# Level 0 of a triangular inverse moved from its own code into the loop over levels, with the side work re-placed

## The reference, cut to what matters

```python
def step(S, inp):
    r_t, w_t, k_t, v_t, kk_t, a_t = inp
    s_kk = jnp.einsum('zbhvk,zbhk->zbhv', S, kk_t)
    S = (S * w_t[..., None, :] - s_kk[..., None] * (kk_t * a_t)[..., None, :]
         + v_t[..., :, None] * k_t[..., None, :])
    return S, jnp.einsum('zbhvk,zbhk->zbhv', S, r_t)
```

```python
y = (y - mu) * lax.rsqrt(var + GN_EPS) * heads(gn_w.astype(f32)) + heads(gn_b.astype(f32))
out = ((y + bonus).reshape(B_, L, D_A) * gate).astype(h.dtype)
```

## Time and profile before

| what | value |
|---|---|
| median of three runs | 2405.79 us |
| the profiled execution's own time | 2401.35 us |
| its span | 2399.4 us |
| mean granted clock of TensorE | 0.983 |
| PE busy | 2243.7 us (94%) |
| DVE busy | 936.9 us (39%) |
| ACT busy | 397.0 us (17%) |

### The profile page before, as it was taken

The page is one execution under the profiler, slowest core; times in us unless marked ns, Lnnn a source line. Parts: engine busy times, 40 slices in busy tenths (PEclk is TensorE's granted clock), DMA queues, the critical chain, the costliest instruction groups (busy, mean ns, idle before and its releaser), DMA issues. The chain is left out here.

```text
span 2399.4 us, 56100 instructions
## 1 busy us (share of the span) xinstructions
PE 2243.7 (94%) x23412; PEld 1282.6 (53%) x23412; DVE 936.9 (39%) x1965; ACT 397.0 (17%) x685; POOL 167.3 (7%) x162
## 2 busy tenths in 40 slices
PE   5998989999888889999999999889998999999997
PEld 2446777777676765544444444545555444444444
DVE  2357666676757621211111111479613111111113
ACT  2022323232323201000000000211312000000001
POOL 1001010100101000000000000000000000000000
PEclk8998999999999999999999999899999999999999
DMA  9981010101000035799999999502036999999995
GB/s 369 386 316 32 2 33 2 32 2 32 13 22 21 2 122 197 268 383 393 395 396 393 394 396 390 193 1 70 1 140 255 395 397 394 393 397 393 392 392 172
DMA packets 181670, 538.56 MB, mean 224 GB/s; under 512 B 12545, under 2 KB 54145, under 8 KB 181410
## 3 DMA queue, kind: packets, MB, share of 16 engines
q1 hardware_dynamic: 175202, 515.16, 55.8%
q0 software_dynamic: 6336, 21.63, 3.8%
HBM read 510.81 MB, written 25.95 MB: 224 GB/s over the span
## 5 line engine op out<-in xcount | busy, mean ns | idle before, releaser
L2108 PE MATMUL ps<-raw,xs 128*64 128x512 f32 x3072 | 673.8, 596 | 4.0 <-PEq L2102 3.9
L2108 PEld LDWEIGHTS ps<-raw,xs 128*64 128x64 f32 x3072 | 217.7, 137 | 431.0 <-issue 429.6
L2120 PE MATMUL ps<-raw,xs 128*32 128x256 f32 x6144 | 342.3, 380 | 3.2 <-PEq L2102 3.2
L2120 PEld LDWEIGHTS ps<-raw,xs 128*32 128x32 f32 x6144 | 195.1, 110 | 134.0 <-issue 10.4
L2299 DVE SCALAR_TENSOR_TENSOR h<-h,ps 128x768 f32<-128x768 f32 x32 | 30.5, 954 | 461.9 <-DVEq L2298 461.9
L1644 DVE COPY_PREDICATED wk<-m,ps 128x128 f32<-128x128 uint8 x360 | 101.4, 352 | 116.4 <-DVEq L1640 116.2
L2426 PE MATMUL ps<-h,raw 128*128 128x512 f32 (+1 forms) x448 | 124.7, 440 | 7.2 <-PEq L2417 7.2
L2227 ACT ACTIVATE h<-ps 128x768 f32<-128x768 f32 x32 | 25.9, 811 | 595.1 <-ACTq L2226 595.1
L900 PE MATMUL ps<-h,wk 128*128 128x512 f32 (+1 forms) x416 | 121.4, 438 | 1.5 <-PEq L1216 1.3
L1030 PE MATMUL ps<-wk 64*64 64x64 f32 x2400 | 102.9, 223 | 14.5 <-PEq L1006 13.8
L1044 PE MATMUL ps<-wk 64*64 64x64 f32 x2400 | 98.5, 219 | 5.0 <-PEq L1006 3.2
(11 more groups left out here) (333 smaller groups left out, 2643.9 us busy)
## 6 DMA issues: line engine op xcount, KB each, us to landing
raw<-in_moe_w_gate SPq DMA_DIRECT2D x64, 2048.0 KB, 18.0
raw<-in_moe_w_up SPq DMA_DIRECT2D x64, 2048.0 KB, 20.0
raw<-in_moe_w_down SPq DMA_DIRECT2D x64, 2048.0 KB, 19.1
wk<-in_mod_w SPq DMA_DIRECT2D x24, 2048.0 KB, 12.1
wk<-in_ev_w_in SPq DMA_DIRECT2D x18, 512.0 KB, 5.3
raw<-in_od_w_in SPq DMA_DIRECT2D x4, 2048.0 KB, 15.2
hrow<-rows SPq DMA_DIRECT2D x10, 512.0 KB, 2.9
ysum<-low SPq DMA_DIRECT2D x10, 512.0 KB
```

Of the source, the lines that this page charges most:

```text
L2108: last = pe.matmul(ps[to:to + CAPS, bank_of(kind, ee)], XS[ee][:, c, 0:CAPS], raw[:, slot(l, 2 * m + c // 4), c % 4, 8 * to:8 * to + 512], ...
L2120: last = pe.matmul(ps[to:to + 32, bank_of(kind, ee) + 1, 0:256], XS[ee][:, c, CAPS:], raw[:, slot(l, 2 * m + c // 4), c % 4, 8 * to:8 * to ...
```

## The change

Level 0 loses its own code. The loop on PE has five turns, for levels 0 to 4, and each turn has 128 tokens of `keys`; so `keys(ST)` moves from ahead of the loop to its last turn. Ahead of the loop stand now only the first three `middle`, which at level 0 multiply with the identity. ACT makes 35 copies of `yw` instead of 30. The wait for the identities moves from DVE to PE, ahead of the first `middle`, and DVE gives the first turn its four counts of `x_new` at once. `TAIL` is spread over levels 0 to 4. For the last pair, and only there, each step of the tail stands behind every third tile (q = 2, 5, ... 23) and not behind the fifth tile of a level.

```diff
--- before.py
+++ after.py
@@ -818,7 +818,7 @@
             halves = ((0, NS), (NS, T))
             Q, K, VV = 0, 1, 2
             QUERY_ENDS = (0, 3, NT)
-            TAIL = ((0, 1), (2, 3), (4, 5), (6,), (7,), ())
+            TAIL = ((0,), (1, 2), (3, 4), (5,), (6, 7), ())
 
             def cells_of(ap, j):
 
@@ -1005,22 +1005,6 @@
 
                             pe.wait_ge(sem(name), n).then_inc(sem(name), -n)
 
-                        def diagonal(ap, lo, hi):
-
-                            return ap[lo:hi, :, :, 0, lo:hi].rearrange("p z h n -> p (z h) n")
-
-                        def first_correct(g):
-
-                            zb = zbank(g)
-                            for k, (lo, hi) in enumerate(HALF):
-                                to, te = HALF[1 - k]
-                                pe.matmul(ps[to:te, zb, 0:4 * HD].rearrange("p (u n) -> p u n", u=4), eye64[lo:hi], diagonal(mat[:, g], lo, hi), start=True, stop=True)
-                            for z in range(2):
-                                for hh in range(2):
-                                    for lo, hi in HALF:
-                                        last = pe.matmul(ps[lo:hi, zb + 1, slotN(z, hh):slotN(z, hh) + HD], mat[lo:hi, g, z, hh, 0, lo:hi], eye64[lo:hi], start=True, stop=True)
-                            last.then_inc(sem("z_ready"), 1)
-
                         def correct(g, both=True):
 
                             zb = zbank(g)
@@ -1064,29 +1048,21 @@
 
                         def keys(tt):
 
-                            at = slice(tt * P, tt * P + P) if isinstance(tt, int) else bass.ds(tt * P, P)
+                            at = bass.ds(tt * P, P)
                             for c in range(KC):
                                 last = pe.matmul(pair(0)[:, at], win[:, c, K], h[:, c, at], start=c == 0, stop=c == KC - 1)
                             last.then_inc(sem("keys_ready"), 1)
 
-                        first_correct(0)
-                        first_correct(1)
+                        pe.wait_ge(sem("invT_reset"), 1).then_inc(sem("invT_reset"), -1)
                         pe.wait_ge(sem("yvar_read"), 1).then_inc(sem("yvar_read"), -1)
+                        middle(0)
+                        middle(1)
                         pe.wait_ge(sem("r_copied"), 1).then_inc(sem("r_copied"), -1)
                         if following:
                             take_weights()
-                            keys(ST)
-                        take("x_new", 2)
-                        first_correct(2)
-                        middle(0)
-                        take("x_new", 2)
-                        first_correct(3)
-                        middle(1)
-                        take("x_new", 2)
-                        first_correct(4)
                         take("yw_copied", 1)
                         middle(2)
-                        with pe.Fori(0, LEVELS - 2) as lev:
+                        with pe.Fori(0, LEVELS - 1) as lev:
                             take("x_new", 4)
                             correct(0)
                             take("yw_copied", 1)
@@ -1330,11 +1306,11 @@
                         y_root()
                         act.sem_inc(sem("yvar_read"), 1)
                         copy_r(0, 1)
-                        for u in range(NZ):
-                            g, w = u % NT, 4 * HD if u < NZ - NT else 2 * HD
+                        for u in range(NZ + NT):
+                            g, w = u % NT, 4 * HD if u < NZ else 2 * HD
                             act.wait_ge(sem("yw_ready"), 1).then_inc(sem("yw_ready"), -1)
                             act.activation(yw[:, g].rearrange("p z h n -> p (z h n)")[:, 0:w], ps[:, mbank(g), 0:w], ACT.Copy).then_inc(sem("yw_copied"), 1)
-                            if u == NZ - NT - 1:
+                            if u == NZ - 1:
                                 act.wait_ge(sem("tail_done"), 1).then_inc(sem("tail_done"), -1)
                                 if following:
                                     copy_raw(K, 0, parts=NT)
@@ -1634,7 +1610,7 @@
                                     n += 1
                             if tt == 0:
                                 old_states()
-                        dve.wait_ge(sem("invT_reset"), 1).then_inc(sem("invT_reset"), -1)
+                        dve.sem_inc(sem("x_new"), 4)
                         for q in range(NZ):
                             g = q % NT
                             dve.wait_ge(sem("z_ready"), 1).then_inc(sem("z_ready"), -1)
@@ -1646,9 +1622,11 @@
                             if q >= NZ - NT:
                                 done(2)
                                 dve.sem_inc(sem("x_new"), 2)
-                            if g == NT - 1:
+                            if following and g == NT - 1:
                                 for k in TAIL[lev]:
                                     tail(k, i)
+                            if not following and q % 3 == 2 and q < 24:
+                                tail(q // 3, i)
                         for lo, hi in ((0, HD), (HD, P)):
                             for g in range(NT):
                                 dve.tensor_copy(mat[lo:hi, g, :, :, 0, lo:hi], xx[P - hi:P - lo, g, :, 0]).then_inc(dve_done, 1)
```

## The result

The changed kernel takes 2418.22 us, the median of five runs from 2414.87 to 2420.30, against 2405.79 us, the median of five runs too (2401.39 to 2407.46). The ratio is 1.0052 with a 95% interval from 1.0037 to 1.0067: 12.4 us slower, where 9.5 us slower was forecast. The profiled execution took 2414.87 us.

A forecast was written before the change was run, and what follows sets the result against it. PE was taken as nearly the bound, DVE and ACT hidden where order allows. Five pairs' 6.5 us plus the last pair's 3.0 gave 9.5 us, median 2405.79 to 2415 us; own range 2410.5 to 2420, 8 in 10 from 2407 to 2423.

The forecast's parts named there:

- The start: From PE's start of a pair to DVE's first masked copy: 2.77 us where it was 0.94, 1.8 us later.
- Five turns: Loop in each of the first five pairs: five full turns with `keys` at 7.20 us each, 36.0 us.
- The tail under `keys`: Joint of two levels: two reciprocals take 2.41 us and fit within 0.1 us; without cover one costs 1.2 us.
- The last pair: Window without `keys`: start 2.77, turns 28.5 and tail 4.1 us, 35.37 us against 32.33, so 3.0 us more.
- bare turns: Last pair's turns without tail steps: 5.85 us at levels 0 and 1, then 5.63, last 5.5; together 28.5 us.
- the tail's 4.1 us: Last pair: tail steps among the copies delay them by 4.1 us, between 0 and 8.7 us.
- Code loading: PE's stalls on code not loaded: 3.9 us for five pairs as before, no change; bounds 3.9 us less, 9 us more.
- The rival that the slack holds: Last pair's tail costs nothing, 4.1 us less, and code stalls go, 3.9 us less: 2407 us, no difference; chance 0.15.
- a stall in every first pass: Loop body's first pass stalls at every pair, 1.3 to 2.6 us each: 2419 to 2424 us; chance 0.14.
- a faster kernel: Shorter straight code saves one load per pair, up to 3.0 us each, 18 us over six: 2397 us; chance 0.06.
- The signs of being wrong: First turns under 7 us, third and fourth pair's windows not longer, or last pair's reciprocals leaving no gap on PE.
- the loop's jump back: Each turn reloads the loop's head, one more load per pair at 1.0 to 2.6 us: 2421 to 2431 us; chance 0.03.

The follow-up runs named there:

- Number 3: The changed kernel with ACT's first copy of `yw` ahead of its copy of the old state's product, PE's wait moved behind the loop; 2419.20 us in one run.
- number 7: The changed kernel with 32 idle matmuls on PE ahead of all pairs, which only move the code behind them; 2413.14 us in one run.
- number 1: The changed kernel with the last pair's tail by the table, behind the fifth tile of a level as in the other pairs; 2413.21 us in one run.
- number 4: The kernel before with only the changed kernel's `TAIL` table, for all six pairs; level 0 keeps its own code; 2399.94 us in one run.
- number 5: The kernel before with a `TAIL` table that leaves level 0 without any tail; 2402.30 us against 2405.97, ratio 0.9981.
- number 6: The kernel before with only `keys(ST)` moved from ahead of the loop to behind its last turn; 2412.11 us in one run.
- number 2: The changed kernel with the last pair's eight tail steps all behind level 5; 2427.22 us in one run.

## Why the prediction was right

The sign, the place and most of the size were right: windows 10.2 us longer, forecast 9.5. By its parts, the first five pairs are 7.6 us longer for 6.5 and the last 2.6 for 3.0, so a small miss one way met a small one the other way.

- **The start.** Forecast 2.77 us, measured 2.90 us in all six pairs, 2.0 us over 0.94 and 11.8 us over six. The chain's events come in the order that was argued; the third `middle` was under-sized, 0.35 us to the next instruction for 0.3, and DVE's first copy comes 0.94 us behind `correct(0)` for 0.87. Number 3 shows that the state's copy is not the whole reason: without it in the way the start is still 2.65 us, where 2.0 was expected. The 0.3 us for a `middle` was wrong ahead of the loop, where one takes 0.57 us. That the forecast came out so close in spite of it is luck in part: the state's copy covers the slow product, with 0.25 us to spare.
- **Five turns.** Forecast 36.0 us, measured 36.1 us in the two clean pairs, the third of number 7 (7.24, 7.32, 7.12, 7.22 and 7.20 us) and the fifth of number 1. Against 36.50 us for the same stretch of the kernel before this gives 0.4 us back per pair. So a clean pair is 1.5 us longer, forecast 1.3. In the changed kernel itself the turns take 36.3 to 36.6 us in three pairs and, with the longer waits for code, 37.4 and 37.6 us in two.
- **The tail under `keys`.** Two reciprocals behind level 1 were to fit within 0.1 us; 7.31 us for 7.2 shows it. What one costs without that cover was put at its whole 1.2 us. Numbers 4 and 5 show 0.15 us for a first and 1.3 us for a second: the joint ahead of level 1 had room for one.
- **The last pair.** Forecast 35.37 us, measured 34.97, of which some 0.6 us are a wait for code that the forecast did not have there; without one it is 34.36 us (number 7), so that wait made the forecast look closer. (In the kernel before, the window of 32.33 us has two short waits, 0.18 and 0.36 us; the last pair of number 6, with the same code and no wait, takes 32.04 us. So without waits the last pair is 2.3 us longer, forecast 3.0.) The bare turns came as forecast (number 2: 5.86, 5.63, 5.62 and 5.61 us for 5.85, 5.63, 5.63 and 5.5). The step that failed is the tail's 4.1 us, which is 2.6 us by the measured difference and 2.9 us by the clean pair. Level 1 with its two reciprocals takes 7.29 us, 1.4 us over the bare turn, for 1.85 in the sum and a turn of about 7.7 us in the forecast of the profile; step 0 costs 0.2 us for 0.65. By DVE's rows in number 2 the copies behind a delayed one follow each other without gap, so a delay in the middle of a level is made good before its end. The argument that a block in the joint has 1.0 us free that single steps have not falls by number 1: 0.2 us.
- **Code loading.** Forecast 3.9 us for five pairs, as before; it is 3.9 us, in other pairs. That it fits so closely is chance: with the same loop it was 2.4 us in number 1 and 5.5 us in number 2. The rival that the slack holds, chance 0.15, falls by this and by the tail's 2.6 us. The fear of a stall in every first pass, chance 0.14, fell. The chance of 0.06 for a faster kernel rested on fewer code loads. They did become fewer: from the start of the first window to 900 us queue 8 brings 46 instruction packets, and 51 before. The waits for code did not shrink with them, so a load is not as such on PE's path.
- **Outside the windows.** The median moved by 12.4 us, the windows by 10.2. The other 2 us are within what the rest of the kernel varies by from profile to profile, and within the interval, 8.9 to 16.1 us. What varies there was not tried.
- **The range.** The bounds as they were given, all at their low or high end, reach from 2405 to 2423 us (1.0 us off or 0.5 us on six times, 4 or 4.6 us for the last tail). The 2410.5 to 2420 us on record are narrower than that and don't follow from them. And a stall of 1.3 to 2.6 us in five pairs would be 2.6 to 9.1 us over the 3.9 already in the sum, not 4 to 9. Neither changes which side the result falls on.

The signs of being wrong did not come: the first turns take 7.42 us or more in the five pairs with `keys`, the third and fourth window are 3.0 and 1.9 us longer (with waits for code in the third), and in the last pair PE waits 1.54 us for DVE's copy behind level 1's second reciprocal.

For a pair with `keys` the change has three parts, and two were run alone. The new table takes 0.7 us off a clean pair (number 4), moving `keys` adds 0.4 to 0.6 us (number 6). If they simply add, and that was not tried, taking level 0 into the loop costs the rest, 1.7 to 1.9 us in a clean pair, which is near the 2.0 us of the later start. So the re-placed tail is a gain that hides part of the cost.

One rival rested on the loop's jump back. In the second pair the loop jumps back three times from 350 us on; PE's matmuls go from `keys` to `correct(0)` at about 353, 360 and 367 us. The changed kernel's DMA traffic from 350 to 377.2 us:

```profile
DMA packets 0, 0.00 MB, mean 0 GB/s; under 512 B 0, under 2 KB 0, under 8 KB 0
```

No packet comes, so none of these jumps loads code. The Trainium skill, page Runtime: NRT & Kernel Launch, section Instruction fetch mechanics, says that a taken branch to a target outside the current window of two pages forces a fetch. Whether this trace contradicts it hangs on how much a page holds. An estimate from the trace: from 336.26 to 451.70 us the second pair has 3957 records of matmuls and loads. Four of its five turns, 2048 of these records, repeat a body that is already there; the other 1909 came with eight packets of queue 8, some 240 a packet. If a packet is a page, the body's 512 records, besides its waits, are more than two, and the trace doesn't agree with the rule for PE. Either way the rival, 6 to 16 us slower, did not come.

## What to carry to other kernels

A special first step that skips a product can be worth more than the product's own time: it also saves the chain through the other engines ahead of the first result, 2 us here, and here this was paid in each of the six pairs, as the code starts anew. Side work for a waiting engine belongs where another engine's work covers its whole length: here two reciprocals cost about 0.1 us under `keys`, and without that cover the second one cost 1.3 us. A loop's turn can be priced from its steady state, but its first one has to be built from its chain.

## What I had not expected of the hardware

PE waits for code in the middle of dense code. In the third pair of the changed kernel the instruction packet of 0.02 MB starts at 454.9 us and PE goes on at 457.12, 2.2 us later and 1.3 us after the packet has ended; over all 57 waits it is 1.26 to 1.55 us from the packet's end. Places in the stream decide where PE waits, for 0.2 to 2.0 us at a time, but how long varies from run to run. Two `middle` alone take 0.07 us for an fp32 matmul of 64x64 (16 in 1.15 us) where a whole turn's mix of both takes 0.04 us (24 matmuls in 0.93 us).
